# A hand-planned two-layer kernel on Trainium2: products with transposed blocks move to the head of the next transposes, and some low parts move to VectorE

## What is computed

```
h = rmsnorm(x, norm1_g);  p = h @ w_in
a_out = pool_mixer(...)
b_out: 4 heads, (softmax(q1 k1^T) - lam * softmax(q2 k2^T)) v, causal
c_out: 4 heads, z = q k^T / 8
       A = exp(log_sigmoid(z) + suffix sum of log_sigmoid(-z)), strictly causal;  out = A v
x = x + concat(a_out, b_out, c_out) @ w_out
h2 = rmsnorm(x, norm2_g)
x = x + (silu(h2 @ w_gate) * (h2 @ w_up)) @ w_down
return rmsnorm(x, final_norm_g)
```

## Time and profile before

| | |
|---|---|
| median of 3 runs | 3668.71 us (3667.5 to 3670.57) |
| profiled execution, its own time | 3671.6 us |
| span of its profile | 3669.8 us |
| PE busy in the span | 3625.8 us (99%) |
| DVE, ACT, POOL busy | 2036.2, 1506.8, 685.0 us |
| granted PE clock, mean | 0.996 |

### The profile page before, as it was taken

How to read it: one execution, slowest core, us unless ns; L and a number is a source line. 1 busy time by engine, 2 the same in 40 slices (tenths; PEclk the granted TensorE clock), 3 DMA queues, 4 the chain that set the end, 5 groups by cost and what they waited for, 6 DMA issues and landing times. The chain is left out here.

```text
span 3669.8 us, 62811 instructions
## 1 busy us (share of the span) xinstructions
PE 3625.8 (99%) x25608; PEld 3129.8 (85%) x25608; DVE 2036.2 (55%) x3851; ACT 1506.8 (41%) x2751; POOL 685.0 (19%) x407
## 2 busy tenths in 40 slices
PE   9999999999999999999999999999999999999999
PEld 7889888978897988987788888888877899998998
DVE  4757635551645354557655665555566465546555
ACT  3332431231232364566656665444555422223222
POOL 2001130000000000233333321000000254415442
PEclk9999999999999999999999999999999999999999
DMA  7746687557655977876776665554533666666664
GB/s 300 284 179 247 241 303 252 202 208 241 221 219 190 284 254 239 291 239 223 246 235 220 228 239 181 166 169 149 173 139 119 224 252 235 233 232 232 234 235 184
DMA packets 215534, 820.57 MB, mean 224 GB/s; under 512 B 22096, under 2 KB 71504, under 8 KB 152144
## 3 DMA queue, kind: packets, MB, share of 16 engines
q1 hardware_dynamic: 215248, 816.57, 62.9%
HBM read 615.15 MB, written 201.33 MB: 222 GB/s over the span
## 5 line engine op out<-in xcount | busy, mean ns | idle before, releaser
L1671 PE MATMUL bank<-slot,Z0b 128*128 128x512 f32 (+1 forms) x3504 | 703.6, 352 | 2.2 <-DVE R L2522 2.2
L1671 PEld LDWEIGHTS bank<-slot,Z0b 128*128 128x128 f32 x3504 | 559.8, 188 | 92.7 <-DVE R L2522 3.9
L1671 PE MATMUL bank<-Z1a,slot 128*128 128x512 f32 (+1 forms) x2568 | 603.8, 379 | 7.1 <-POOL slot L3144 5.5
L1671 PE MATMUL bank<-Z1b,slot 128*128 128x512 f32 (+1 forms) x2568 | 604.5, 379 | 0.9 <-DVE Z1b L2569 0.9
L1671 PEld LDWEIGHTS bank<-Z1a,slot 128*128 128x128 f32 x2568 | 445.3, 189 | 94.8 <-POOL slot L3144 4.5
L1671 PEld LDWEIGHTS bank<-Z1b,slot 128*128 128x128 f32 x2568 | 444.5, 189 | 89.0 <-issue 4.1
L3144 POOL TENSOR_TENSOR slot<-raw,slot 128x1024 fp32r<-128x1024 f32 x110 | 272.6, 2486 | 698.3 <-ACT slot L2170 698.3
L2522 DVE SCALAR_TENSOR_TENSOR R<-bank,small,R 128x512 f32<-128x512 f32 x352 | 261.3, 748 | 174.6 <-PE bank L1671 174.1
L2875 DVE TENSOR_SCALAR_CACHE_REDUCE P<-bank 128x512 f32<-128x512 f32 (+3 forms) x320 | 189.0, 608 | 228.0 <-PE bank L1671 227.2
L3162 POOL TENSOR_TENSOR Z0b<-AF,Z0b 128x512 fp32r<-128x512 f32 x88 | 134.3, 1526 | 792.8 <-ACT Z0b L2360 792.8
L1671 PE MATMUL bank<-KS,DQ 128*128 128x512 f32 (+3 forms) x960 | 275.9, 387 | 5.6 <-DVE P L2875 2.0
(11 more groups left out here) (267 smaller groups left out, 5506.7 us busy)
## 6 DMA issues: line engine op xcount, KB each, us to landing
slot<-Wd SPq DMA_DIRECT2D x350, 1024.0 KB, 5.6
Wd<-slot SPq DMA_DIRECT2D x130, 1024.0 KB, 7.7
raw<-in_wts_dram SPq DMA_DIRECT2D x210, 512.0 KB, 4.7
DQ<-Qd SPq DMA_DIRECT2D x192, 128.0 KB, 3.9
slot<-Wd SPq DMA_DIRECT2D x40, 512.0 KB, 6.6
DV<-Vd SPq DMA_DIRECT2D x60, 256.0 KB, 4.8
KS<-Kd SPq DMA_DIRECT2D x24, 512.0 KB, 7.0
KS<-Kd SPq DMA_DIRECT2D x24, 384.0 KB, 7.0
```

The costliest lines, as they stand in the source:

```text
L1671: return e.matmul(o, a, b, start=start, stop=stop, skip_group_check=True)
```

## The change

In `back`, groups are now taken by twos over the whole list of units. For each two, the products that are still owed (`pend`, from the two before, also across the end of a unit) are put first, and right behind them the transposes of the new two; both wait, in the plan, for the later of everything they need: the combining of the new two, the copies to TP and the values of the old two, and the two buffers in use. What comes after a unit's last product (`o`, `finish_diff`, `finish_stick`, the loads of the next values) goes with that product. In `split_weights`, tiles of the first block's projections (j < N_A) also go to DVE where DVE's clock in the plan is less than 1,100 ns behind the later of the tile's arrival and POOL's clock.

```diff
--- before.py
+++ after.py
@@ -313,7 +313,8 @@
 
     def split_weights(self, j):
         lo = ("pool", 2400)
-        if j < NSLOT or self.taps:
+        P = self.P
+        if j < NSLOT or self.taps or j < N_A and P.clock["dve"] < max(P.end["wf", j], P.clock["pool"]) + 1100:
             self.on_dve.add(("w", j))
             lo = ("dve", 1220)
         return self.P.put(("w", j), ("act", 1060), lo, after=self.P.end[("wf", j)])
@@ -776,5 +777,6 @@
     def back(self):
         P = self.P
         yield ("att",)
+        pend = []
         for u, (s, e, half, qt) in enumerate(self.units):
             i = self.heads.index((s, e))
             if (half, qt) == (0, 0):
@@ -784,43 +789,42 @@
                     yield ("norms done",)
                 for g in range(s + 1):
                     self.get(i, ("v", g))
-            nb = NT * s + qt + 1
+            gs = groups_in_order((s, e, half, qt))
+            for two in [gs[x:x + 2] for x in range(0, len(gs), 2)]:
+                k = ("cb", u) if e < 4 else ("cp", u, piece_of((s, e, half, qt), two[-1]))
+                yield k
+                yield max([P.end[k], self.values_at(pend)] + [P.end[x] for x in self.tp_uses[-2:]])
+                self.values(pend)
+                pend = []
+                for g in two:
+                    w = min(4, blocks_of((s, e, half, qt)) - 4 * g)
+                    self.tp_uses.append(("tr", u, g))
+                    t = P.put(("tr", u, g), ("pe", 107 * w), ("act", 200 + 108 * w), after=P.end[k])
+                    pend.append((u, g, w, t))
+        yield self.values_at(pend)
+        self.values(pend)
+
+    def values_at(self, groups):
+
+        return max([0.0] + [max(t, self.P.end["ld", self.heads.index(self.units[u][:2]), "v", g]) for u, g, w, t in groups])
+
+    def values(self, groups):
+
+        P = self.P
+        for u, g, w, t in groups:
+            s, e, half, qt = self.units[u]
+            i = self.heads.index((s, e))
             last = qt == NT - 1 and (half == 1 or e < 4)
-            pend = []
-            for g in groups_in_order((s, e, half, qt)):
-                k = ("cb", u) if e < 4 else ("cp", u, piece_of((s, e, half, qt), g))
-                yield k
-                m = len(self.tp_uses)
-                if m > 1:
-                    yield P.end[self.tp_uses[m - 2]]
-                yield P.end[k]
-                w = min(4, nb - 4 * g)
-                self.tp_uses.append(("tr", u, g))
-                t = P.put(("tr", u, g), ("pe", 107 * w), ("act", 200 + 108 * w), after=P.end[k])
-                if e < 4 and pend:
-                    yield from self.av(u, i, pend, last)
-                    pend = []
-                pend.append((g, w, t))
-                if len(pend) == 2:
-                    yield from self.av(u, i, pend, last)
-                    pend = []
-            if pend:
-                yield from self.av(u, i, pend, last)
-            if e < 4:
-                P.put(("o", u), ("act", 540), after=P.clock["pe"] + 200)
-            else:
-                P.put(("o", u), ("act", 280), ("dve", 280), after=P.clock["pe"] + 200)
-            if last:
-                P.add(self.finish_diff(i, s, e) if e < 4 else self.finish_stick(i, s, e), slack=SLACK_C)
-
-    def av(self, u, i, groups, last):
-
-        yield max(max(t, self.P.end["ld", i, "v", g]) for g, w, t in groups)
-        s, e = self.heads[i]
-        for g, w, t in groups:
-            self.P.put(("av", u, g), ("pe", (215 if e < 4 else 110) * w), after=max(t, self.P.end[("ld", i, "v", g)]))
+            P.put(("av", u, g), ("pe", (215 if e < 4 else 110) * w), after=max(t, P.end["ld", i, "v", g]))
             if last:
                 self.get(i + 1, ("v", g))
+            if g == groups_in_order((s, e, half, qt))[-1]:
+                if e < 4:
+                    P.put(("o", u), ("act", 540), after=P.clock["pe"] + 200)
+                else:
+                    P.put(("o", u), ("act", 280), ("dve", 280), after=P.clock["pe"] + 200)
+                if last:
+                    P.add(self.finish_diff(i, s, e) if e < 4 else self.finish_stick(i, s, e), slack=SLACK_C)
 
     def finish_diff(self, i, s, e):
         P = self.P
```

## The result

| | before | with the change |
|---|---|---|
| median | 3669.6 us (4 runs) | 3698.0 us (4 runs, 3694.8 to 3702.8) |
| ratio | | 1.0077, 95% interval 1.0059 to 1.0094 |
| span of the profile | 3669.8 us | 3695.4 us |
| PE busy, idle in the span | 3625.8, 44.0 us | 3632.4, 63.0 us |

The change makes the kernel 28 us slower. The forecast was 3662 us, the range ended at 3673, and slower had a chance of 0.11.

A forecast was written before the change was run, and what follows sets the result against it. PE, busy 99% of the span, was taken as the bound. Terms of 2.3 + 1.1 + 0.8 + 2.7 = 6.9 us off 3671.6 gave 3664.7; with the median 2.9 lower, 3662 us, range 3652 to 3673.

The forecast's parts named there:

- Borders: PE's exits from stick products: 47 more lead into transposes, each saving 0.05 us; 2.3 us off, bounds 0 and 5.2.
- drained-all-the-same rival: Stick products' exits save nothing, as a change of tiling mode drains the engine anyway; 3664 us, chance 0.05.
- Start wait: PE's wait before tile 6 shortens as DVE, not POOL, makes its low halves; 1.1 us off.
- Start clock: Half clock behind the start's wait loses 1.7 us in place of 2.5; 0.8 off, ends 0 and 2.5.
- Attention's waits: Waits at 1602 and 2254 us go, 8.7 off, and 6.0 of new ones come; 2.7 us off.
- Late products: In attention `o`, loads of next values and heads' ends come one unit later; costed at nothing.
- slower rival: Merged runs of s = 2 and 3: late second TP copies hold up PE, 2.66 us each; six give 3678, chance 0.08.

The follow-up runs named there:

- e8: changed kernel, but diff units' owed products put at their unit's end, only stick products held over to the next unit; 3673.3 us, ratio 1.0007.
- e11: e10 with the back lane's slack (`SLACK_B`) at 2600 ns for 2500; 3671.4 us, ratio 1.0001.
- e1: kernel before with only the edit in `split_weights`, back lane as before; 3668.2 us, ratio 0.9992.
- e14: changed kernel with early loads of values moved behind the products they wait for, only products at diff heads' ends held over; 3690.5 us.
- e13: changed kernel with early loads of values moved behind their products, and one row block of the last norm behind three bank copies; 3686.5 us.
- e15: changed kernel with early loads of values moved behind their products, only products of diff units that end no head held over; 3716.8 us.
- e6: kernel before with the back lane's slack (`SLACK_B`) at 2700 ns for 2500; 3689.4 us, ratio 1.0054.
- e3: changed kernel, but all products owed at a unit's end put there, none held over; 3676.4 us, ratio 1.0014.
- e5: kernel before with the back lane's slack (`SLACK_B`) at 2400 ns for 2500; 3669.7 us, ratio 1.0000.
- e10: e8 with the ten loads of values that stood too early moved behind the products they wait for; 3675.8 us, ratio 1.0014.
- e16: e1 with two `norm2` stages moved in the finished list, s = 0 behind copies to TP and Z1b, s = 1 earlier; 3663.7 us.
- e2: changed kernel without the edit in `split_weights`, only the new back lane; 3699.8 us, ratio 1.0081.

## Why the prediction was wrong, step by step

- **Borders, 2.3 us off: not shown.** In the changed kernel twelve stick products take 2853.15 - 2852.34 = 0.81 us and the eight transposes behind them 2854.00 - 2853.15 = 0.85:

```profile
2852.34 0.88 PE L1675 MATMUL bank<-TP,DV 128*64 128x128 f32 x12
2853.15 1.09 PE L1679 MATMUL bank<-pvt,P 128*128 128x128 f32 x8
2854.00 0.70 PE L1675 MATMUL bank<-KS,DQ 128*128 128x512 f32 x2
```

  The 0.85 us is what was forecast, but a saving should show in PE's busy time. Less what half speed lost, that was 3615.7 us before and 3620.3 with the change, 3615.9 in e8 and 3615.4 in e11, which both keep the joined runs of stick heads. A saving of 2.3 us is not seen there, nor can these sums, which move by more than that for other reasons, exclude it; the drained-all-the-same rival (0) stands.
- **Start wait, 1.1 off: right** (4.05 to 2.89 us, forecast 2.9 to 3.0). POOL has 102 and DVE 28 low parts, as said. Tile 4 still waits for POOL, 1.15 us for 1.48.
- **Start clock, 0.8 off: 2.5 in the changed kernel,** the stated end of the range, and 0.9 in e1, which still lost 1.6.
- **Attention's waits, 2.7 off: this step failed, by 22 us of idle time.** I called the waits at 1602 and 2254 us gone. The wait at OR did shrink, to 0.58, but table loads still stood in front of other work that PE needed, and PE waited 1.27 and 2.63 us within 6 us of it, with a half clock as before:

```profile
1602.62 0.63 PE L1679 MATMUL bank<-pvt,OR 128*128 128x128 f32 x4 [0.58 <-DVE OR L2949]
1604.52 0.92 PE L1675 MATMUL bank<-KS,DQ 128*128 128x512 f32 x3 [1.27 <-DVE P L2879]
...
1608.37 2.92 PE L1675 MATMUL bank<-Z1b,slot 128*128 128x512 f32 x6 [2.63 <-DVE Z1b L2573]
```

  At 2254 us the wait for GS is gone, and one of 2.28 us for Z1b stands at 2267. New waits were set at 6.0 us, by the old order's count of two, and without a half clock; idle time rose by 19.5, and half speed cost attention some 9 us where it had cost 4.5.
- **Late products, costed at nothing: the root.** Putting the diff products back at their unit's end takes 25 us off (e8 against the changed kernel). "A load has a whole unit of time" was wrong twice. The load is put a unit ahead of the product it waits for, so what has no time is all that stands behind it on SP's queue (the 4.1 us at 2576); and with one buffer of values a later last product shortens the load's own time (14.6 us of waits in e14). I had counted the instructions that move on PE, ACT and DVE, and not looked at where the loads stood on SP's queue.
- **The slower rival** was on the right side with the wrong place: TP waits are 1.2 us in all. Its kind, table loads in front of something that is waited for, is what stood at 2188 us, on DVE's way to the banks, and went in e13.

What stays open: e13 is still 16 us over the kernel before. Left in it are waits of 3.5 us at 2630, 2.6 at 1611 and 2.3 at 2266 us, three of 9.6 us together in front of products with values, and the half clocks behind them. I took none of these away one by one. What the inner diff units cost in the changed kernel is not settled either, as e15's own plan is so much longer. How the 28 us divide among the queue of loads, the values' own time and the waits for ACT and DVE is not known. A second buffer of values was not tried.

## What to carry to other kernels

When a piece of work is put later, list what is issued in its name on every queue, the DMA queue first, and see whether it now stands ahead of what it waits for: an in-order queue makes its wait everyone's. Where the plan leaves out a cost (table loads here), a wait that a new order takes away in one place can stand again a few us further on, as at 1602 us. Read the plan's own end before a new order runs: one constant made it 16.7 us longer in e6, which then lost 19. But a plan that is no longer (2.9 us here) is no promise, since it leaves out what cost the 28 us. A small gain at borders should be set against the few us that kernels with nothing held over differ by (3668 to 3676 us in e1, e3, e5, e8, e10 and e11). Moving one stage in the finished list is a cheap and sharp test of one wait, and the fastest version (e16) was made in that way.

## What the runs showed of the hardware

The same wait does not always cost the same clock, in one profiled execution of each kernel. The wait of 2.28 us before Z1b's products had no half clock behind it in the changed kernel and one in e2, which has the same back lane and differs in the low parts; the windows of the changed kernel and then of e2, columns as in rows 3:

```profile
2267.00:2273.00 6.00, 5.59 (x22) 4.25 (x23) 5.54 (x6) 2.63 (x5) 2.40 (x1) 1.00 0.46 156
```

```profile
2270.00:2273.40 3.40, 3.37 (x8) 2.69 (x9) 3.37 (x2) 2.28 (x4) 2.17 (x1) 0.52 0.00 0
```

The wait of 2.89 us at the start did the same, in e1 and in the changed kernel. So the price of a wait of 2 to 3 us was its length alone, or 1.6 to 1.7 us more (half of the 3.37 us busy in e2's window, a third of the 4.77 in e1's).
